# A batched triangular inverse on one core: 64x64 matmuls on whole blocks against 32x32 matmuls on packed diagonal blocks

## The reference, cut to what matters

```python
def step(S, inp):
    r_t, w_t, k_t, v_t, kk_t, a_t = inp
    sa = jnp.einsum('bhvk,bhk->bhv', S, kk_t)
    S = (S * w_t[:, :, None, :]
         - sa[..., None] * (kk_t * a_t)[:, :, None, :]
         + v_t[..., None] * k_t[:, :, None, :])
    y = jnp.einsum('bhvk,bhk->bhv', S, r_t)
    return S, y
```

## Time and profile before

| | us |
|---|---|
| median of 3 runs | 2605.02 (2600.08 to 2606.02) |
| the profiled execution, its own time | 2608.94 |
| its span in the trace | 2607.2 |
| PE busy | 2495.6 (96%) |
| DVE busy | 1580.5 (61%) |
| ACT busy | 1166.0 (45%) |
| POOL busy | 191.0 (7%) |

### The profile page before, as it was taken

The page is one execution under the profiler, slowest core; times in us unless marked ns, Lnnn a source line. Parts: engine busy times, 40 slices in busy tenths (PEclk is TensorE's granted clock), DMA queues, the critical chain, the costliest instruction groups (busy, mean ns, idle before and its releaser), DMA issues.

```text
span 2607.2 us, 53930 instructions
## 1 busy us (share of the span) xinstructions
PE 2495.6 (96%) x22769; PEld 2372.7 (91%) x22769; DVE 1580.5 (61%) x1766; ACT 1166.0 (45%) x1433; POOL 191.0 (7%) x149
## 2 busy tenths in 40 slices
PE   6889999999999999999999999999999999999998
PEld 4889998899898989999989999999999888999886
DVE  5687745664757445555678987555665544455444
ACT  3444433232335444666465434536554433444442
POOL 4053302430000000000000000000000000000000
PEclk8889999999999999999999999999999999999999
DMA  6346454221254555445545656455566555666554
GB/s 191 130 138 210 150 191 139 80 80 57 100 194 153 185 187 185 147 152 188 172 139 178 183 165 178 153 183 166 161 186 194 184 188 186 186 185 185 186 186 136
DMA packets 219205, 426.00 MB, mean 163 GB/s; under 512 B 17136, under 2 KB 21312, under 8 KB 218288
## 3 DMA queue, kind: packets, MB, share of 16 engines
q1 hardware_dynamic: 213984, 403.59, 49.1%
q0 software_dynamic: 3296, 14.26, 1.6%
q10 hardware_dynamic: 1728, 5.24, 0.5%
HBM read 414.66 MB, written 8.39 MB: 162 GB/s over the span
## 4 chain that ended last, share of the span: by engine, by line
PE 84%; DVE 9%; ACT 3%; POOL 2%; issue 2%; DMA 1%; SPq 0%; DVEq 0%; ACTq 0%; POOLq 0%
PE ps L493 25%; PE ps L494 24%; PE ps L495 24%; PE ps L696 6%; DVE wlo L333 2%; ACT whi L329 1%; POOL M L420 1%; POOL M L422 1%; PE ps L746 1%; DVE act_lo L1477 1%; DMA M<-gate_input_scratch 1%; PE ps L604 0%; DVE regions L1490 0%; DVE act_lo L1768 0%; PE ps L846 0%
## 5 line engine op out<-in xcount | busy, mean ns | idle before, releaser
L333 DVE TENSOR_TENSOR wlo<-wraw,whi 128x1024 fp32r<-128x1024 f32 x752 | 951.8, 1271 | 855.3 <-ACT whi L329 854.1
L493 PE MATMUL ps<-act_hi,whi 128*128 128x256 f32 (+1 forms) x4736 | 1359.5, 287 | 33.5 <-DVE act_lo L1879 12.9
L494 PE MATMUL ps<-act_lo,whi 128*128 128x256 f32 (+1 forms) x4736 | 1344.3, 284 | 0.0
L495 PE MATMUL ps<-act_hi,wlo 128*128 128x256 f32 (+1 forms) x4736 | 1342.4, 283 | 0.0
L329 ACT ACTIVATE whi<-wraw 128x1024 fp32r<-128x1024 f32 x752 | 793.7, 1059 | 1158.3 <-PE ps L495 1143.5
L493 PEld LDWEIGHTS ps<-act_hi,whi 128*128 128x128 f32 x4736 | 903.8, 191 | 41.1 <-issue 26.9
L494 PEld LDWEIGHTS ps<-act_lo,whi 128*128 128x128 f32 x4736 | 906.5, 191 | 0.6
L495 PEld LDWEIGHTS ps<-act_hi,wlo 128*128 128x128 f32 x4736 | 903.2, 191 | 0.0
L494 PE MATMUL ps<-wlo,regions_r 128*128 128x512 f32 x512 | 203.0, 396 | 0.0
L495 PE MATMUL ps<-whi,regions_r 128*128 128x512 f32 x512 | 203.0, 396 | 0.0
L493 PE MATMUL ps<-whi,regions_r 128*128 128x512 f32 x512 | 203.0, 396 | 0.0
(11 more groups left out here) (305 smaller groups left out, 1718.6 us busy)
## 6 DMA issues: line engine op xcount, KB each, us to landing
wraw<-in_a_w_in SPq DMA_DIRECT2D x128, 512.0 KB, 4.6
wraw<-in_w_up SPq DMA_DIRECT2D x128, 512.0 KB, 3.9
wraw<-in_w_down SPq DMA_DIRECT2D x128, 512.0 KB, 4.5
wraw<-in_w_in SPq DMA_DIRECT2D x112, 512.0 KB, 3.8
wraw<-in_b_w_qg SPq DMA_DIRECT2D x64, 512.0 KB, 3.7
wraw<-in_a_w_out SPq DMA_DIRECT2D x32, 512.0 KB, 4.0
wraw<-in_w_k_shared SPq DMA_DIRECT2D x32, 512.0 KB, 4.4
wraw<-in_w_v_shared SPq DMA_DIRECT2D x32, 512.0 KB, 4.6
```

What stands on the lines that cost most here:

```text
L333: nc.vector.tensor_tensor(wlo[:, q % RING], wraw[:, q % RING], whi[:, q % RING].bitcast(F32), ALU.subtract).then_inc(lo_ready, 1)
L493: mm(o, hi_s, hi_m, start=first, stop=False, skip_group_check=True)
L494: mm(o, hi_s, lo_m, start=False, stop=False, skip_group_check=True)
L495: i = mm(o, lo_s, hi_m, start=False, stop=last, skip_group_check=True)
```

## The change

For levels 0 to 4 only the two 32x32 diagonal blocks of each head are kept. The two heads and two blocks of a column group lie on the four quarters of the partitions, so a head pair takes 32 columns in place of 64, and a half f takes 256 columns in place of 512 (`ABd`, `Bm`, `Tp`, `Tm`, `Yl`).

- PE: `y` and `z` of levels 1 to 4 are `small_pairs`: 32 matmuls of 32 rows, 32 columns and 32 moving columns each, four in turn on the four quarters. `y` and `z` of level 5 are `cross_pairs`: 16 matmuls of 32x32 by 32 for the one off-diagonal block, two in turn. `ab` stays.
- DVE: after `AB`, one more instruction packs its diagonal blocks into `ABd`. All operations of `pair` and of `z` work on 256 columns; the last subtraction writes the off-diagonal quarter of `TTs`.
- ACT: the copy to `Yl` has 256 columns. At level 5 it also spreads `Tp` over `TTs` in two instructions per half f, with factors 1, 0 by partition.
- POOL: masks 256 columns, five levels in place of six for each chunk and half (40 instructions in place of 48).
- Waits: ACT's copy now waits for the last `z` of its half (`lv_z`) in place of `lv_t`; DVE's `pair` of a later chunk and its last subtraction wait for ACT's spreading (`tt_half`); the scan waits for `tt_ready`.
- The constants shrink from six masks of 64 columns to five masks of 32, an identity of 32 and three columns.

The core of the diff:

```diff
+        ABd, Bm, Tp, Tm, Yl = (R[:, 1, 1024 + 512 * i:1536 + 512 * i] for i in range(5))
...
+            def small_pairs(f, o_bank, lhs, rhs):
+
+                for j in range(8 * f, 8 * f + 8):
+                    at = slice(j * HB, (j + 1) * HB)
+                    for r0 in range(0, P, HB):
+                        m_ = mm(ps[r0:r0 + HB, o_bank, (j % 8) * HB:(j % 8 + 1) * HB], lhs[r0:r0 + HB, at], rhs[r0:r0 + HB, at],
+                                start=True, stop=True)
+                return m_
+
+            def cross_pairs(f, o_bank, lhs, rhs, down):
+
+                for j in range(8 * f, 8 * f + 8):
+                    for hs in (0, N):
+                        i0, o0 = (hs, hs + HB) if down else (hs + HB, hs)
+                        m_ = mm(ps[o0:o0 + HB, o_bank, (j % 8) * HB:(j % 8 + 1) * HB], lhs(slice(i0, i0 + HB), j), rhs(slice(i0, i0 + HB), j),
+                                start=True, stop=True)
+                return m_
...
                 if kind == "y":
-                    pe.wait_ge(S["lv_b"], n_ + 1)
-                    pe.wait_ge(S["lv_m"], m_ + 1)
-                    pairs(f, 4 + f, (flat(Bm), flat(Tm))).then_inc(S["lv_y"], 1)
+                    pe.wait_ge(S["lv_m"], LV_T(c, f, lv - 1))
+                    if lv < 5:
+                        pe.wait_ge(S["lv_b"], LV_T(c, f, lv))
+                        m_ = small_pairs(f, 4 + f, Bm, Tm)
+                    else:
+                        m_ = cross_pairs(f, 4 + f, lambda r_, j: AB[r_, j * CH + HB:(j + 1) * CH], half(Tm), True)
+                    m_.then_inc(S["lv_y"], 1)
                 if kind == "z":
-                    pe.wait_ge(S["lv_ysb"], m_ + 1)
-                    pe.wait_ge(S["lv_t"], n_ - 1)
-                    pairs(f, 6 + f, (tt_, flat(Yl)) if lv < 5 else (flat(Yl), tt_)).then_inc(S["lv_z"], 1)
+                    pe.wait_ge(S["lv_ysb"], LV_Y(c, f, lv))
+                    pe.wait_ge(S["lv_t"], LV_T(c, f, lv - 1))
+                    m_ = small_pairs(f, 6 + f, Tp, Yl) if lv < 5 else cross_pairs(f, 6 + f, half(Yl), half(Tp), False)
+                    m_.then_inc(S["lv_z"], 1)
...
+                    act.wait_ge(S["lv_y"], LV_Y(c, f, lv))
+                    if c or lv > 1:
+                        act.wait_ge(S["lv_z"], LV_Y(c, f, lv - 1) if lv > 1 else LV_Y(c - 1, f, 5))
+                    st.do(a(Yl[:, f * 256:(f + 1) * 256], half_at(4 + f, 0), ACT.Copy), sig["lv_ysb"])
+                    if lv == 5:
+                        act.wait_ge(S["lv_t"], LV_T(c, f, 4))
+                        whole = TTs[:, c, f * GW:(f + 1) * GW].rearrange("p (h b t) -> p h b t", h=8, b=2)
+                        for b in range(2):
+                            st.do(a(whole[:, :, b, :], blocks(Tp, f), ACT.Copy, scale=cs("halves")[:, b:b + 1]), sig["tt_half"] if b else None)
...
                     st.do(tt(heads(AB[:, fs], 8), heads(bank(4 + f), 8), cs("causal")[:, 0:CH].unsqueeze(1).broadcast_to([P, 8, CH]),
-                             ALU.mult), sig["ab_ready"])
+                             ALU.mult))
+                    st.prev()
+                    both = AB[:, fs].rearrange("p (h b t) -> p h b t", h=8, b=2)
+                    st.do(stt(blocks(ABd, f), both[:, :, 1, :], lower, both[:, :, 0, :], ALU.mult, ALU.add), sig["ab_ready"])
...
+                    st.do(tt(blocks(Tm, f), blocks(Tm, f), half_at(6 + f, 1), ALU.subtract), sig["lv_m"])
                     st.prev()
-                    st.do(nc.vector.transpose(TTs[:, c, fs], Tm[:, fs]), sig["lv_t"])
+                    st.do(nc.vector.transpose(Tp[:, 256 * f:256 * (f + 1)], Tm[:, 256 * f:256 * (f + 1)]), sig["lv_t"])
```

More of the change, by code:

```diff
@@ L27 @@
 CH = 64
+HB = 32
 LORA = 96
@@ L57, in constants @@
     parts["causal"] = np.concatenate([(s < t), (s <= t)], 1) * 1.0
-    for lv in range(6):
+    s32, t32 = (p % HB)[:, None], np.arange(HB)[None, :]
+    for lv in range(5):
         m = 1 << lv
-        parts[f"level{lv}"] = ((s // (2 * m) == t // (2 * m)) & ((t // m) % 2 == 1) & ((s // m) % 2 == 0)) * 1.0
+        parts[f"level{lv}"] = ((s32 // (2 * m) == t32 // (2 * m)) & ((t32 // m) % 2 == 1) & ((s32 // m) % 2 == 0)) * 1.0
+    parts["ident32"] = (s32 == t32) * 1.0
+    parts["halves"] = np.stack([p % CH < HB, p % CH >= HB, -1.0 * (p % CH < HB)], 1) * 1.0
     parts["restart"] = np.tile((np.arange(T)[None, :] % CH != 0) * 1.0, (P, 1))
@@ L248, in program @@
         TTs = R[:, 0, :].rearrange("p (c n) -> p c n", c=4)
-        AB, Bm, Tm, Yl = (R[:, 1, 1024 * i:1024 * (i + 1)] for i in range(4))
+        AB = R[:, 1, 0:1024]
+        ABd, Bm, Tp, Tm, Yl = (R[:, 1, 1024 + 512 * i:1536 + 512 * i] for i in range(5))
         AM = wk(0, 3072).rearrange("p (j a t) -> p j a t", j=KT, a=3)
@@ L266, in program @@
                     level_steps += [("z", c, f, lv)] + [("ab", c + 1, f, 0)] * (lv == 5 and c < 3)
+        LV_T = lambda c, f, lv: (c * 5 + lv) * 2 + f + 1
+        LV_Y = lambda c, f, lv: (c * 5 + lv - 1) * 2 + f + 1
+        blocks = lambda t_, f: t_[:, 256 * f:256 * (f + 1)].rearrange("p (h t) -> p h t", h=8)
+        half_at = lambda b, n: ps[:, b, 0:256].rearrange("p (h t) -> p h t", h=8) if n else ps[:, b, 0:256]
         steps_at, at_ = [], 0
@@ L442, in _ @@
             for c in range(4):
-                for lv in range(6):
+                for lv in range(5):
                     for f in range(2):
-                        n_ = (c * 6 + lv) * 2 + f
                         if lv == 0:
@@ L448, in _ @@
                         if lv == 0 and c:
-                            pool.wait_ge(S["lv_y"], (c * 5 - 1) * 2 + f + 1)
+                            pool.wait_ge(S["lv_y"], LV_Y(c - 1, f, 4))
                         if lv == 1:
-                            pool.wait_ge(S["lv_t"], n_ - 1)
+                            pool.wait_ge(S["lv_t"], LV_T(c, f, 0))
                         if lv >= 2:
[L453 to L456, removed]
+                            pool.wait_ge(S["lv_y"], LV_Y(c, f, lv - 1))
+                        ptt(blocks(Bm, f), blocks(ABd, f), cs(f"level{lv}").unsqueeze(1).broadcast_to([P, 8, HB]), ALU.mult).then_inc(S["lv_b"], 1)
             pool.wait_ge(S["bv_stored0"], 32)
@@ L735, in _ @@
             pe.wait_ge(S["silu_ready"], 4)
-            pe.wait_ge(S["lv_t"], 48)
+            pe.wait_ge(S["tt_ready"], 8)
             for it in range(4):
@@ L1102, in level @@
                 if kind == "y":
-                    n_, m_ = (c * 6 + lv) * 2 + f, (c * 5 + lv - 1) * 2 + f
-                    if n_ < 4:
+                    if c == 0 and lv == 1:
                         act.wait_ge(S["bv_stored1"], 32)
-                    act.wait_ge(S["lv_y"], m_ + 1)
-                    act.wait_ge(S["lv_t"], n_ - 1)
-                    st.do(a(Yl[:, f * GW:(f + 1) * GW], bank(4 + f), ACT.Copy), sig["lv_ysb"])
+                    act.wait_ge(S["lv_y"], LV_Y(c, f, lv))
[7 more added lines that the diff above has]
+                            st.do(a(whole[:, :, b, :], blocks(Tp, f), ACT.Copy, scale=cs("halves")[:, b:b + 1]), sig["tt_half"] if b else None)
             for s in range(4):
@@ L1601, in gn_part2 @@
                       sig["yn_ready"])
-            i8 = cs("ident64").unsqueeze(1).broadcast_to([P, 8, CH])
+            i8 = cs("ident32").unsqueeze(1).broadcast_to([P, 8, HB])
+            upper, lower, less = (cs("halves")[:, i:i + 1] for i in range(3))
             def level(kind, c, f, lv):
-                n_, m_ = (c * 6 + lv) * 2 + f, (c * 5 + lv - 1) * 2 + f
                 fs = slice(f * GW, (f + 1) * GW)
@@ L1612, in level @@
                     st.do(tt(heads(AB[:, fs], 8), heads(bank(4 + f), 8), cs("causal")[:, 0:CH].unsqueeze(1).broadcast_to([P, 8, CH]),
-                             ALU.mult), sig["ab_ready"])
+                             ALU.mult))
+                    st.prev()
+                    both = AB[:, fs].rearrange("p (h b t) -> p h b t", h=8, b=2)
+                    st.do(stt(blocks(ABd, f), both[:, :, 1, :], lower, both[:, :, 0, :], ALU.mult, ALU.add), sig["ab_ready"])
                 if kind == "pair":
-                    if c == 0 and f == 0:
+                    if c:
+                        dve.wait_ge(S["tt_half"], 2 * c - 1 + f)
+                    elif f == 0:
@@ L1616, in level @@
                         dve.wait_ge(S["bv_stored0"], 32)
-                    dve.wait_ge(S["lv_b"], n_ + 1)
-                    st.do(tt(heads(TTs[:, c, fs], 8), i8, heads(Bm[:, fs], 8), ALU.subtract), sig["lv_t"])
+                    dve.wait_ge(S["lv_b"], LV_T(c, f, 0))
+                    st.do(tt(blocks(Tp, f), i8, blocks(Bm, f), ALU.subtract), sig["lv_t"])
                     st.prev()
-                    st.do(nc.vector.transpose(Tm[:, fs], TTs[:, c, fs]), sig["lv_m"])
+                    st.do(nc.vector.transpose(Tm[:, 256 * f:256 * (f + 1)], Tp[:, 256 * f:256 * (f + 1)]), sig["lv_m"])
@@ L1626, in level @@
                 if kind == "z" and lv == 5:
-                    dve.wait_ge(S["lv_z"], m_ + 1)
```

(5 more changed lines are left out.)

10 lines of the change are left out of this document (4 added, 6 removed).

## The result

The changed kernel takes 2618.1 us (median of 7 runs, 2611.7 to 2620.5) against 2605.0 before: a ratio of 1.0046 with an interval of 1.0031 to 1.0061, some 12 us slower. The forecast was 2581, and 2561 to 2606 as the range.

What follows compares the result with a forecast made beforehand. PE was taken to bound the kernel. 12.8 + 3.2 + 9 - 1 = 24 us less took the profiled 2608.9 to 2584.9 and the median to 2581 us; range 2561 to 2606, at 0.80.

Steps and rivals of the forecast that it cites:

- The bound: PE, busy for 2495.6 of 2607.2 us, sets the end; only its own time or its waits count.
- Part 1: Products of levels 1 to 4, 64 groups: 0.94 to 0.74 us each, 12.8 us less, between 25.6 and nothing.
- part 5: Work of ACT, DVE, POOL, new waits and faster slab demand: covered behind PE, with no term in the sum.
- Part 2: Products of level 5, 16 groups: 0.94 to 0.74 us each, 3.2 us less, between 6.4 and 0.
- Part 3: First chunk and changes of chunk: shorter masks and `pair` take back 9 us of 15, ends 4 and 12.
- Part 4: Six added changes of tile size within bursts, some 0.1 us each: 1 us lost.
- The number of starts decides: Rival, 0.15, slower: PE's records have their own price whatever the tile, in `small_pairs`; 22 us more, 2627.
- A new wait takes the gain: Rival, 0.08: PE waits for `Tm` in short bursts, up to 1.2 us in 16 levels, 19 us of 24; 2600.
- What would show it wrong: Profile signs: bursts over 2.1 us, PE idle before z or y on ACT or DVE, POOL waits as before.

Runs made afterwards that it cites:

- run with half of the products: Changed kernel with every second head pair left out of the 32x32 products of levels 1 to 4, masks and spreading factors zero: 2556.3 us.
- half-packed one: Changed kernel with only f = 0 packed; f = 1 keeps 64x64 blocks up to level 4, with the off-diagonal level 5: 2595.0 us, ratio 0.9957.
- run with the quarters outside: Changed kernel with the loop over the four quarters outside, a quarter's eight products one after the other, same instructions: 2715.8 us.
- light loads: Changed kernel with only 64 of 512 columns of each weight slab of projection g loaded: 2609.4 us.
- run with one column: Changed kernel with one moving column in place of 32 in the small products of levels 1 to 4, masks and spreading factors zero: 2623.8 us.

## Why the prediction was wrong, point by point

*The bound.* Right that PE sets the end. But the argument asked only which engine's work or wait ends last, and never what brings PE its instructions. With 152 instructions per 3.61 us before, a block of 256 lasted 6.1 us, and nothing showed.

*Part 1, the small products.* The array's part was right, and better than taken: 9.1 ns from start to start (11.5 taken, 8.5 the low end), 0.58 us a group. That is 64 x (0.94 - 0.58) = 23 us gained at the full clock. Four quarters in turn do start faster than two (9.1 against 16.2 ns). What the prediction took from the columns isn't shown: tile and columns changed together, and at this tile one column in place of 32 saves 0.5 ns of 9.1.

*The step that failed* is part 5, "what is covered". It lists ACT, DVE, POOL, SP and the slabs, and costs 4096 further PE instructions (2048 matmuls and their loads) at nothing beyond the array. They need 16 blocks more, in a place where a block comes every 3.5 to 5.5 us (median 3.9) and would be used up in 3.0. Waits of 23 us before L714 and some 9 us before other PE lines are "issue" in this stage, 31.8 in all, where the kernel before had none. They alone take back nearly all that the other parts gave. The run with half of the products (3.2 us before L714) and the half-packed one (2.9 before its 64x64 products), both of which use up 256 instructions in 3.9 to 4.0 us, lose nearly all of these waits.

*Part 2, level 5.* A group and the `ab` group behind it at the full clock:

```profile
458.05 0.69 PE L723 MATMUL ps<-regions 32*32 32x32 f32 x32
458.67 1.15 PE L702 MATMUL ps<-regions 64*64 64x64 f32 x32
```

(0.69 - 0.19)/31 is some 16.2 ns from start to start, 0.52 us a group: the low end, 7 us of gain, confirmed alone by the 7.5 us of the run with level 5 only.

*Part 3, the changes of chunk.* POOL's mask takes 0.65 us undisturbed, as taken. y(1) waits for POOL 0.75 and 0.26 us in the timeline of PE, against 1.21 and 0.57:

```profile
463.63 0.74 PE L714 MATMUL ps<-regions 32*32 32x32 f32 x64 [0.75 <-POOL regions L462]
464.63 0.74 PE L714 MATMUL ps<-regions 32*32 32x32 f32 x64 [0.26 <-POOL regions L462]
```

So about 1 us of wait stays in a change, as predicted, against 1.8 before. But the term of 9 us was too large: the waits for POOL fell by 2.9 us in the whole stage, from 8.6 to 5.7. The 9 us counted ways of 12.3 us that were long also by a granted clock of 0.86, as if the chain alone had made them. After the change the last of the three ways has 0.82 again and takes 12.4 us; the first two, at the full clock, take 8.9.

*Part 4, changes of tile size,* was right: from one start to the other in the two rows of part 2 it is 0.62 us, of which 31 distances are 0.50, so a change costs about 0.1 us.

*A term that the sum lacked, the clock.* The granted clock fell more often than before: 0.77 from 434.99 to 442.48 us above, which begins with the end of a wait of 1.36 us, and in the whole stage, from its first `ab` product to the scan's first (before, then after):

```profile
407.24:602.99 195.75, 184.98 (x3498) 175.02 (x3497) 117.00 (x126) 59.20 (x74) 68.13 (x48) 0.97 0.28 94
...
405.76:613.19 207.43, 167.75 (x5545) 154.92 (x5545) 84.89 (x134) 56.01 (x90) 31.31 (x40) 0.92 0.28 89
```

These two rows give the account. The stage is 11.7 us longer: 31.8 us of "issue" more, 2.9 us of waits for POOL less, and PE's busy time 17.2 us less. At the full clock the busy time should have fallen by 23 + 7 = 30 us, so 13 us are missing. The clock can be up to 11 of them (an estimate from the rows, 207.43 x 0.08 - 195.75 x 0.03). So supply took back the gain, and the slower clock is most likely why the kernel is slower than before and not the same. Why the clock fell is open. Waits can't be the whole reason: in the run with the quarters outside it fell with PE busy nearly throughout.

*The rivals.* "The number of starts decides" had the right side and the right place, and its price from which it decides, 16.7 ns, is passed: with 280 instructions in 4.02 us and 1.75 us for the rest, a record of `small_pairs` costs (4.02 - 1.75)/128 = 17.7 ns. But its mechanism is another: the price is not that of a start (9.1 ns in a burst) but that of a block. And the floor of 25 ns cited beside it from the Trainium skill ("TensorE: Matmul & The Clock Gate", "Back-to-back issue gap") does not hold between matmuls on four quarters, which start every 9.1 ns here. (By the prediction's own sum that floor gives 42 - 8 = 34 us, not 32 to 33; and its high end puts part 3 at 8 us where the text has 9. Neither matters.) "A new wait takes the gain" was right only in that waits took it: in regular levels DVE and ACT were never late. At the first chunk and the changes of chunk PE's weight loads also waited for DVE's transpose (L1658), 6.7 us.

*What would show it wrong* named bursts over 2.1 us, waits on ACT, DVE or POOL. Idle time with "issue" as releaser, the one that came, was not on the list.

## What to carry to other kernels

Count the instructions of a stretch, not only their work: here 256 instructions of one engine (127 matmuls with their loads) need 3.3 us at the least to be delivered and 3.9 as a rule, with hardly any other traffic too, so a change that cuts work per instruction pays only until that rate is reached. Splitting a product into more and smaller matmuls is then best done in part: half packed was 23 us faster than all packed. Idle time of PE with "issue" as releaser, at the same distance in instructions each time, is how it looks.

## What the runs showed of the hardware that was not expected

- A block of 256 PE instructions, one 16 KB packet, came every 3.5 to 5.5 us where PE waited for it (median 3.9), and every 3.3 to 4.1 with light loads, down to 4 GB/s of traffic. The packet itself takes 0.9 to 1.5 us of that.
- Four 32x32 tiles in turn start a float32 record every 9.1 ns, two every 16.2; the same records tile by tile take 27 ns. The order of the loop decides over a factor of three.
- The granted clock fell to 1.2 GHz (0.50 granted) with very different work: for 14 us after waits of 0.6 to 1.4 us in the run with one column, and for 37 us (563 to 600 us) with PE busy throughout in the run with the quarters outside.
